# Ten of twelve gate chunks a layer as seven half-size products, with weight sums on GpSimd

## The reference, cut to what matters

```python
h = rmsnorm(x, norm_mix_pre[l])
proj = jnp.einsum('bsd,de->bse', h, w_in[l])          # its last 3072 columns are gl
ys = jnp.stack([ya, yb, yc], axis=2)                  # three branches, each 512 wide
z = jnp.einsum('bsnc,ncd->bsnd', ys, w_branch[l])
gates = jax.nn.sigmoid(gl + b_gate[l]).reshape(B, S, N_BRANCH, D_MODEL)
merged = jnp.sum(gates * z, axis=2)
mix = jnp.einsum('bsd,de->bse', merged, w_out[l])
```

## Time and profile before

| what | value |
|---|---|
| median of 3 runs | 3088.75 us (3086.27 to 3090.51) |
| profiled execution, its own time | 3087.93 us |
| its span, first to last instruction | 3086.1 us |
| PE busy | 3055.7 us (99%) |
| DVE, ACT, POOL busy | 1797.3, 1262.2, 173.3 us |
| mean granted TensorE clock | 0.998 |

### The profile page before, as it was taken

The page is one execution under the profiler, slowest core; times in us unless marked ns, Lnnn a source line. Parts: engine busy times, 40 slices in busy tenths (PEclk is TensorE's granted clock), DMA queues, the critical chain, the costliest instruction groups (busy, mean ns, idle before and its releaser), DMA issues.

```text
span 3086.1 us, 41574 instructions
## 1 busy us (share of the span) xinstructions
PE 3055.7 (99%) x16571; PEld 2508.3 (81%) x16571; DVE 1797.3 (58%) x2460; ACT 1262.2 (41%) x1788; POOL 173.3 (6%) x227
## 2 busy tenths in 40 slices
PE   8999999999999999999999999999999999999999
PEld 7767888888887688888888678888888888888887
DVE  3673446557755634655578866557743333465576
ACT  3563234335544622433365254336521221343355
POOL 2030000000021200000001100000000000000000
PEclk9999999999999999999999999999999999999999
DMA  6206853224542188232253147987423323332244
GB/s 181 66 28 224 193 143 110 95 95 143 167 93 79 60 252 194 96 109 95 95 191 110 56 170 198 298 192 219 150 91 109 110 82 110 103 109 95 95 136 157
DMA packets 298859, 408.96 MB, mean 133 GB/s; under 512 B 19925, under 2 KB 211453, under 8 KB 298461
## 3 DMA queue, kind: packets, MB, share of 16 engines
q1 hardware_dynamic: 251164, 306.75, 30.5%
q0 software_dynamic: 47552, 100.21, 13.7%
HBM read 400.54 MB, written 90.18 MB: 159 GB/s over the span
## 4 chain that ended last, share of the span: by engine, by line
PE 88%; DVE 8%; ACT 2%; DMA 2%; issue 1%; DVEq 0%; SPq 0%; ACTq 0%
PE ps L1980 20%; PE ps L1982 19%; PE ps L1981 19%; PE ps L2130 4%; PE ps L2131 4%; PE ps L2132 4%; PE ps L2082 2%; PE ps L2084 2%; PE ps L2083 2%; DMA t_wraw<-in_w_in_dram 2%; DVE t_wlo L1289 1%; PE ps L2191 1%; DVE t_vb L1809 1%; PE ps L2564 1%; PE ps L2562 1%; PE ps L2563 1%
## 5 line engine op out<-in xcount | busy, mean ns | idle before, releaser
L1980 PE MATMUL ps<-t_hh,t_whi 128*128 128x512 f32 (+1 forms) x2720 | 1014.9, 373 | 7.0 <-DVE t_hl L1376 4.2
L1982 PE MATMUL ps<-t_hh,t_wlo 128*128 128x512 f32 (+1 forms) x2720 | 1005.0, 369 | 0.0
L1981 PE MATMUL ps<-t_hl,t_whi 128*128 128x512 f32 (+1 forms) x2720 | 1005.0, 369 | 0.0
L1289 DVE TENSOR_TENSOR t_wlo<-t_wraw,t_whi 128x2048 fp32r<-128x2048 f32 x198 | 453.8, 2292 | 790.2 <-ACT t_whi L819 790.2
L819 ACT ACTIVATE t_whi<-t_wraw 128x2048 fp32r<-128x2048 f32 x198 | 379.4, 1916 | 1045.3 <-PE ps L1982 819.7
L1980 PEld LDWEIGHTS ps<-t_hh,t_whi 128*128 128x128 f32 x2720 | 513.3, 189 | 109.5 <-issue 21.1
L1981 PEld LDWEIGHTS ps<-t_hl,t_whi 128*128 128x128 f32 x2720 | 513.5, 189 | 86.8 <-issue 2.4
L1982 PEld LDWEIGHTS ps<-t_hh,t_wlo 128*128 128x128 f32 x2720 | 513.4, 189 | 86.9
L2130 PE MATMUL ps<-t_whi,t_ah 128*128 128x512 f32 x528 | 206.0, 390 | 0.0
L2132 PE MATMUL ps<-t_whi,t_al 128*128 128x512 f32 x528 | 205.5, 389 | 0.0
L2131 PE MATMUL ps<-t_wlo,t_ah 128*128 128x512 f32 x528 | 205.4, 389 | 0.0
(11 more groups left out here) (326 smaller groups left out, 4013.4 us busy)
## 6 DMA issues: line engine op xcount, KB each, us to landing
t_wraw<-in_w_in_dram SPq DMA_DIRECT2D x46, 1024.0 KB, 7.2
t_wraw<-in_w_up_dram SPq DMA_DIRECT2D x44, 1024.0 KB, 5.0
t_wraw<-in_ffn_w_in_dram SPq DMA_DIRECT2D x44, 1024.0 KB, 5.8
t_wraw<-sum_T SPq DMA_DIRECT2D x80, 512.0 KB, 4.2
sum_T<-in_w_down_dram POOLq DMA_DIRECT2D x12, 2560.0 KB, 31.8
sum_T<-in_ffn_w_out_dram POOLq DMA_DIRECT2D x12, 2560.0 KB, 30.9
sum_T<-sum_T POOLq DMA_DIRECT2D x8, 2560.0 KB, 20.3
t_wraw<-in_w_down_dram SPq DMA_DIRECT2D x34, 512.0 KB, 3.6
```

What stands on the lines that cost most here:

```text
L1289: v.tensor_tensor(wlo[slot][:, :], wraw[slot][:, :], whi[slot][:, :].bitcast(F32), ALU.subtract).then_inc(w_lo, 1)
L1980: te.matmul(out, wh, xh, start=first, stop=False)
L1981: te.matmul(out, wh, xl, start=False, stop=False)
L1982: return te.matmul(out, wl, xh, start=False, stop=last)
```

## The change

Ten of the twelve gate chunks of a layer, all but (0,0,0) and (0,0,1), are computed by the Strassen-Winograd scheme. The contraction (1024) is cut into two halves kh, the tokens into two halves th, and the two output tiles of a chunk are the third pair. Instead of eight block products a chunk takes seven, each of 512 of the contraction against 256 tokens: twelve matmuls of 256 tokens. A chunk is then 84 matmuls of 256 tokens instead of 48 of 512.

The operands of the seven products are sums. On the token side T1, T2, T4 and a replaced b12 are made once a layer: two differences of three 128x1024 operations each on POOL (`difference`), four 128x1024 operations on DVE (`rest_of`), then four copies on ACT (`t_high`) and four residuals on DVE (`t_low`). On the weight side POOL makes four sums of 128x512 a chunk, in two buffers that lie in `gain`. The `whi`/`wlo` slots are used as a ring of eight operands of 512 columns: the operand o+8 is made (one 128x512 copy, one 128x512 residual) after product o. The branch chunks go through the same ring as four operands each; their 48 matmuls stay as they are.

The combination of the products costs four copies of 128x256 out of PSUM on ACT for each chunk (`set_aside`), for three of which PE waits before it adds the next product on top, and four operations of 128x256 on DVE (`quarter_out`) in the place of two of 128x512. `gains(2l)` and `weight_sums(l)` move behind the last gate chunk, since `gain` is in use until then. The loops over chunks are unrolled, and branch chunk (0,0) writes banks 4 to 7 in place of 0 to 3.

A group is one pair of gate chunks and its branch chunk: 18 operands, o = 18 gi to 18 gi + 17, five groups a layer. PE's part of the diff:

```diff
-                for j in range(2):
-                    gate_rows(0, 1, j)
-                branch_rows(0, 1)
-                with pe.Fori(1, 3) as n:
-                    for g in range(2):
-                        for j in range(2):
-                            gate_rows(n, g, j)
-                        branch_rows(n, g)
+                def product(o, xh, xl, out, opens, l=l):
+                    wh, wl = op_slot(whi, l, o), op_slot(wlo, l, o)
+                    pe.wait_ge(*op_low(l, o))
+                    for k in range(4):
+                        kk = slice(k * P, (k + 1) * P)
+                        te.matmul(out, wh[:, kk], xh[:, k], start=opens and k == 0, stop=False, skip_group_check=True)
+                        te.matmul(out, wh[:, kk], xl[:, k], start=False, stop=False, skip_group_check=True)
+                        ins = te.matmul(out, wl[:, kk], xh[:, k], start=False, stop=k == 3, skip_group_check=True)
+                    ins.then_inc(op_used(l, o)[0], 1)
+                def split_gate(e, q, i, l=l):
...
+                    product(e, *b11, xx, True)
+                    if e == 0:
+                        pe.wait_ge(t_lo, 4 * l + 4)
+                    product(e + 1, *t1, yy, True)
+                    product(e + 2, *b21, zz, True)
+                    product(e + 3, *t4, ww, True)
+                    pe.wait_ge(x_copied, i + 1)
+                    product(e + 4, *t2, xx, False)
+                    pe.wait_ge(x_copied, i + 2)
+                    product(e + 5, *b22, yy, False)
+                    pe.wait_ge(x_copied, i + 4)
+                    product(e + 6, *b12, xx, False)
```

GpSimd's part:

```diff
                 pool.wait_ge(y_lo, PAIRS[f"A{l}"] + 4)
+                def difference(i, k1, t1, k0, t0):
+                    raw = raw_block(i)
+                    ch.link(gp.tensor_tensor(raw, h_block(hh, k1, t1).bitcast(F32), h_block(hh, k0, t0).bitcast(F32), ALU.subtract))
+                    ch.link(gp.tensor_tensor(raw, raw, h_block(hl, k1, t1).bitcast(F32), ALU.add))
+                    gp.tensor_tensor(raw, raw, h_block(hl, k0, t0).bitcast(F32), ALU.subtract).then_inc(t_sum, 1)
+                difference(2, 0, 1, 0, 0)
+                difference(3, 1, 1, 0, 1)
+                for i in range(2 * GROUPS):
...
+                    pool.wait_ge(w_loaded[cc % 2], (cc // 2 + 1) * 16)
+                    if i:
+                        pool.wait_ge(*op_low(l, before + 5))
+                    gp.tensor_tensor(s1, weight_block(cc, 1, 0), weight_block(cc, 1, 1), ALU.add).then_inc(g_sum, 1)
+                    if i:
+                        pool.wait_ge(*op_low(l, before + 6))
+                    pool.wait_ge(g_sum, n + 1)
+                    gp.tensor_tensor(s2, s1, weight_block(cc, 0, 0), ALU.subtract).then_inc(g_sum, 1)
+                    pool.wait_ge(g_sum, n + 2)
+                    pool.wait_ge(*op_low(l, e + 1))
+                    gp.tensor_tensor(s1, weight_block(cc, 0, 1), s2, ALU.subtract).then_inc(g_sum, 1)
+                    pool.wait_ge(g_sum, n + 3)
+                    pool.wait_ge(*op_low(l, e + 4))
+                    gp.tensor_tensor(s2, weight_block(cc, 0, 0), weight_block(cc, 1, 0), ALU.subtract).then_inc(g_sum, 1)
+                pool.wait_ge(drained, 2 + DRAINS[f"merge{l}"] + 17)
                 gains(2 * l)
                 weight_sums(l)
```

ACT's part (`op_hi(o)` waits for the use of the slot, for the load or the sum, and copies; `set_aside(dst, src, o)` waits for product o):

```diff
+                hi(c)
+                gate(0, 0, 0)
+                act.wait_ge(t_sum, 2 * l + 1)
+                t_high(2, by_k(t1h[:, :]))
+                for o in range(4):
+                    op_hi(o)
+                gate(0, 0, 1)
+                act.wait_ge(t_next, 2 * l + 1)
+                t_high(0, by_k(t2h[:, :]))
+                act.wait_ge(t_next, 2 * l + 2)
+                t_high(1, by_k(t4h[:, :]))
+                act.wait_ge(t_sum, 2 * l + 2)
+                t_high(3, h_block(hh, 0, 1))
+                for o in range(4, 8):
+                    op_hi(o)
+                for gi in range(GROUPS):
+                    n, g = divmod(gi + 1, 2)
                     for j in range(2):
...
+                        set_aside(p1, xx, e)
+                        op_hi(op_next(e))
+                        set_aside(p5, yy, e + 1)
+                        for o in range(e + 1, e + 3):
+                            op_hi(op_next(o))
+                        set_aside(p4, ww, e + 3)
+                        op_hi(op_next(e + 3))
+                        set_aside(u2, xx, e + 4)
+                        for o in range(e + 4, e + 7):
+                            op_hi(op_next(o))
...
+                        gate(n, g, j)
...
+                    for o in range(GROUP_OPS * gi + 14, GROUP_OPS * (gi + 1)):
+                        op_hi(op_next(o))
```

DVE's part:

```diff
+                lo(c)
+                gate(0)
+                t_low(1, 2, by_k(t1h[:, :]), by_k(t1l[:, :]))
+                rest_of(0, 1, 1, 2)
+                dve.wait_ge(t_next, 2 * l + 1)
+                rest_of(1, 1, 0, 0)
+                gate(1)
+                for o in range(4):
+                    op_lo(o)
+                t_low(2, 0, by_k(t2h[:, :]), by_k(t2l[:, :]))
+                t_low(3, 1, by_k(t4h[:, :]), by_k(t4l[:, :]))
+                t_low(4, 3, h_block(hh, 0, 1), h_block(hl, 0, 1))
+                dve.wait_ge(t_lo, 4 * l + 4)
+                weighted_sum(0, 0)
+                for o in range(4, 8):
+                    op_lo(o)
+                for gi in range(GROUPS):
...
+                        for o in range(e, e + 3):
+                            op_lo(op_next(o))
+                        dve.wait_ge(x_copied, i + 1)
+                        dve.wait_ge(*op_used(l, e + 2))
+                        quarter_out(n, g, j, 0, 0, zz, p1)
+                        for o in range(e + 3, e + 6):
+                            op_lo(op_next(o))
+                        dve.wait_ge(x_copied, i + 4)
+                        dve.wait_ge(*op_used(l, e + 5))
+                        quarter_out(n, g, j, 0, 1, yy, u2)
+                        dve.wait_ge(*op_used(l, e + 6))
+                        quarter_out(n, g, j, 1, 1, xx, p5)
+                        quarter_out(n, g, j, 1, 0, xx, p4).then_inc(drained, 1)
+                        op_lo(op_next(e + 6))
...
+                    for o in range(GROUP_OPS * gi + 14, GROUP_OPS * gi + 17):
+                        op_lo(op_next(o))
+                    if gi < GROUPS - 1:
                         weighted_sum(n, g)
+                        op_lo(op_next(GROUP_OPS * gi + 17))
```

160 lines of the change are left out of this document (125 added, 35 removed).

## The result

| | median us | runs | lowest to highest |
|---|---|---|---|
| before | 3089.28 | 4 | 3086.27 to 3090.51 |
| after | 3113.36 | 4 | 3112.79 to 3117.6 |

After is to before as 1.0082 (95% interval 1.0065 to 1.01): 24.1 us slower, where I had forecast 8 and a range that ended at 3108. The execution profiled took 3117.6 us (span 3115.8), 4 above the median.

What follows compares the result with a forecast made beforehand. PE's queue was taken to bound the kernel. A layer: -8.0 - 0.5 (branch chunk's bank wait) + 8.8 + 3.2 + 0.5 = +4.0; two layers +8.0, so median 3097 us, 8-in-10 range 3079 to 3108.

Steps and rivals of the forecast that it cites:

- What PE saves: Gate chunks on PE: seven products of 1.44 us take 10.08 us in place of 10.88, saving 8.0 us a layer.
- The start: Start of each merge: PE waits for token operands made by POOL, DVE and ACT, +8.8 us a layer, bounds 7.3 to 11.3.
- The first group: First group of each merge: products 4 and 6 wait for copies queued on ACT, +3.2 us a layer.
- the clock: Lower PE clock after the start's idle time: up to 1.7 us a layer, hidden by product 4's wait, taken as 0.
- Later groups: Groups after the first: load of the next group's first chunk just fits before product 13, +0.5 us a layer.
- What is moved: Weight-sum DMAs and gain rows issued behind the last gate chunk land well before their first readers: 0 us.
- the lead of the loads: Loads issued early enough hide the weight sums' traffic; without that cover each late load costs what it is late.
- (1): Start of merges hidden, POOL and DVE hardly holding each other up: -5.4 us a layer, kernel 3078; chance 0.22.
- (2): Ring starves in every group: 7.2 us load makes product 13 wait 2.0 us, +16 in all, 3113; chance 0.13.
- (3): Waits and savings cancel: the start of merges costs 5 to 6 us instead of 8.8, 3089 to 3092; chance 0.12.

Runs made afterwards that it cites:

- the combined kernel: Changed kernel with reordered start (both differences on VectorE, queues mended), last group's copies moved, weight sums issued one at a time behind the second handover: 3096.1 us, ratio 1.0013.

## Why the prediction was wrong

The direction was right, and the start of the merges as the largest place of loss; the size, 8 for 24, was not, because the moved transfers, the copies of the last group and the stretch behind the taps were put at nothing. By its own steps:

- **What PE saves**, 8.0 a layer: products without a wait between start 1.44 us apart (in the combined kernel 272.77 to 274.20), as worked out. Right.
- **The start**, +8.8: product 1 starts at 285.66, where 274.25 + 1.1 was due: 10.3 late. Inside the bounds of 7.3 to 11.3. The line of GpSimd and VectorE was somewhat shorter than worked out: the first sum is done at 274.1, not at 275.8. What follows it was longer, 11.5 us for 8.4: GpSimd's second sum did get between and kept VectorE's last pass at 2.2, and VectorE's three `t_low` came behind its four residuals and not behind ScalarE's copies. The slow clock of product 0 has no part in it: product 1 waited another 3.3 us for the last `t_low`, which ends at 285.60.
- **The first group**, +3.2 for products 4 and 6: product 4 was 2.0 later than product 1 makes it, where I had 2.3. It shows as a wait of only 0.49 us, since product 1 ran at the lower clock and used up the rest. The set-aside that product 4 wants ended at 291.92, on a chain from the last `t_low` through the weighted sum, residual 4, GpSimd's fourth sum and operands 6 and 7, none of which waits for these products; so the clock cost nothing here, as forecast. Product 6 did not wait. But products 11 and 13 did, 1.5 and 1.1: together 4.6. I had followed the delay through the first seven products and not through the next.
- **Later groups**, +0.5: 0.4 to 0.5 at each of two products 13 a layer, 0.9 together, and 1.5 at product 4 of the last seven, where the copies of `mg` stand ahead of the set-asides in ScalarE's queue. This step was missing: the change left those lines in place, and I costed only the ones it moved. The sum of a merge is 10.3 + 4.6 + 0.9 + 1.5 - 8.5 = 8.8; measured 8.2 and 9.2, forecast 4.0.
- **What is moved**, 0: wrong, and the step that failed worst. I gave as cover "the lead of the loads" and took it from the merge of before. I also misread its loads: 7.2 us is the median of all 46 loads of `w_in`, and the eight issued in that merge have 13.5. Behind the merge four transfers start at once (DMA 0.88 from 440 to 500), and the four weight loads issued from 440 to 480 took 12.4 to 21.7 us, no longer than in before's merge. But PE waited, since the last load of `w_out` has only 12.9 us of cover. The move alone costs 4.0 us in before; 1.9 and 4.8 are lost in the out stages here. Against that cover I had named its price, "each late load would cost what it is late", without asking which loads would meet the transfers.
- **The rest**, some 5 us: the clock in the convolution module and waits in the up stage behind it, neither touched by the change, repeated in both its profiles. Not foreseen, and the cause stays open.

Of the 16 us between +8 and +24, then, the merges have 9.4 and the out stages 6.7, by landmarks; these sum to 24.1 of the 29.6 between the spans, and the two profiled executions themselves stand 5 further apart than the medians. So how much of the medians' 24.1 the convolution module has is not settled.

**The rivals.** (1), the start hidden: no; operations with two SBUF inputs do hold each other up (1.22 against 2.2 to 3.4, and taking GpSimd out brought 1.22 back). The rule of the Trainium skill (SBUF — State Buffer, "Who interferes with whom") is borne out. (2), the ring starved at every product 13: its 3113 is the time measured, but not by its mechanism; product 13 waits 0.2 to 0.4 in two of the four later groups of a layer and not at all in the others. (3): no.

**Order or work.** The kernel with queues and transfers mended, and six passes moved to VectorE, has all of the change's arithmetic and runs level with before: the ratio goes from 1.0079 to 0.9993, 27 us, of which its profile has 4.6 behind the last tap, in the clock of the convolution module. What stays is 5.2 us of waits a layer in the first group, 7.1 by the distance between starts (272.84 to 300.14 for fourteen products of 1.44), against 8.0 of PE's saving. That this rest is VectorE's throughput is argued from its 27.2 busy us of 30; no run took work off it at that point in the final order.

## What to carry to other kernels

When operands that were loaded are now computed, write each engine's queue out in order as far as the second reuse of every buffer: a set-aside or copy that waits behind an operand "not yet needed" costs as much as the operand, and removing the wait that the profile names may only show the next (products 1, 4, 11, 13 in turn here). Ask of every transfer that is moved which loads it will meet, how many are in flight, how much cover each load has at that place, and who issues them; it may be cheaper issued one at a time. And count no gain from elementwise work on SBUF given to GpSimd while VectorE has two-input work there: here VectorE alone was as fast or faster.

## What the runs showed of the hardware

- A 128x1024 VectorE operation with two SBUF inputs took 1.22 us with GpSimd idle and 2.2, 3.3 or 3.4 beside a GpSimd one; GpSimd's took 2.4 and then 3.25 or 4.33.
- After waits of 5.4 us PE's granted clock was 0.50 for product 0 (starts 0.21 us apart for 0.12); after 3.75 us too its matmuls ran slower for some 6 us (every third start 0.64 us apart, else 0.36; clock 0.50 from 297.8 to 303.8 in the combined kernel). In the merges with no wait above 1.6 us it stayed at 1.00.
- A 2560 KB copy alone in flight landed in 15 to 17 us, one that accumulates in up to 33; four copies issued within 3.3 us landed 19 to 46 us after their issue. A 1 MB load took 5.2 us alone. Medians beside one transfer: 13.2 in the merge, 8.9 in the up stage; beside up to four: 13.5 in before's merge, 19.6 in the up stage.
- A stretch with the same PE work (after the taps) ran at a mean clock of 0.89, 0.83 or 0.77 in profiles of different kernels, 0.77 in both profiles of one, with the edits hundreds of microseconds away.
